# An RWKV-7 scan on one Trainium2 core: two products per step come in the layout of their reader, and the key-side tiles are prepared two steps ahead

## The reference, cut to what matters

```python
def step(S, inp):                       # per head: S is 64 x 64, 16 heads
    r_t, w_t, k_t, v_t, a_t, b_t = inp
    Sa = jnp.einsum('bhvk,bhk->bhv', S, a_t)
    S = S * w_t[:, :, None, :] + Sa[..., None] * b_t[:, :, None, :] + v_t[..., None] * k_t[:, :, None, :]
    y = jnp.einsum('bhvk,bhk->bhv', S, r_t)
    return S, y
_, y = lax.scan(step, S0, (r, w, k, v, a, b))     # 512 tokens
```

## Time and profile before

| | us |
|---|---|
| median of three runs | 1649.29 |
| lowest, highest | 1644.95, 1649.41 |
| the profiled execution's own time | 1648.81 |
| its span in the profile | 1647.0 |
| PE busy (matmuls) | 1545.6, 94% |
| DVE, ACT, POOL busy | 749.6, 586.9, 592.1 |

### The profile page before, as it was taken

How to read it: one execution, slowest core, us unless ns; L and a number is a source line. 1 busy time by engine, 2 the same in 40 slices (tenths; PEclk the granted TensorE clock), 3 DMA queues, 4 the chain that set the end, 5 groups by cost and what they waited for, 6 DMA issues and landing times. The chain is left out here.

```text
span 1647.0 us, 24124 instructions
## 1 busy us (share of the span) xinstructions
PE 1545.6 (94%) x9325; PEld 1205.8 (73%) x9325; DVE 749.6 (46%) x1213; ACT 586.9 (36%) x919; POOL 592.1 (36%) x309
## 2 busy tenths in 40 slices
PE   4699999999899999999999799979999999999998
PEld 3465777777378788888887578745587888888876
DVE  3874969754455320033125773557544310232143
ACT  4655432433333221122234332448442221222242
POOL 4233331110224444434443334244134444344442
PEclk8899999999899999999999999989999999999999
DMA  4121210002212323233323232220022233322331
GB/s 136 51 77 54 92 34 1 3 4 93 79 50 79 102 97 109 92 99 102 103 85 102 78 115 91 77 77 1 1 77 88 91 104 113 102 83 96 102 102 51
DMA packets 123473, 127.33 MB, mean 77 GB/s; under 512 B 8316, under 2 KB 120060, under 8 KB 123384
## 3 DMA queue, kind: packets, MB, share of 16 engines
q1 hardware_dynamic: 122720, 124.90, 23.2%
q0 software_dynamic: 288, 0.59, 0.2%
q10 hardware_dynamic: 376, 0.61, 0.1%
HBM read 123.96 MB, written 2.12 MB: 77 GB/s over the span
## 5 line engine op out<-in xcount | busy, mean ns | idle before, releaser
L439 POOL TENSOR_TENSOR wlo<-wraw,whi 128x1024 fp32r<-128x1024 f32 x108 | 260.6, 2413 | 832.3 <-ACT whi L1223 791.5
L530 PE MATMUL pb<-xh,whi 128*128 128x512 f32 x1184 | 475.7, 402 | 27.9 <-DVE xl L1721 16.3
L531 PE MATMUL pb<-xl,whi 128*128 128x512 f32 x1184 | 464.6, 392 | 0.0
L532 PE MATMUL pb<-xh,wlo 128*128 128x512 f32 x1184 | 464.3, 392 | 0.0
L530 PEld LDWEIGHTS pb<-xh,whi 128*128 128x128 f32 x1184 | 224.2, 189 | 103.4 <-issue 42.3
L1223 ACT ACTIVATE whi<-wraw 128x2048 fp32r<-128x2048 f32 (+1 forms) x111 | 209.2, 1885 | 228.8 <-PE pb L532 223.0
L442 POOL TENSOR_TENSOR wlo<-wraw,whi 128x1024 fp32r<-128x1024 f32 x111 | 274.3, 2471 | 21.1 <-ACT whi L1223 21.1
L531 PEld LDWEIGHTS pb<-xl,whi 128*128 128x128 f32 x1184 | 224.6, 190 | 47.7 <-issue 3.4
L532 PEld LDWEIGHTS pb<-xh,wlo 128*128 128x128 f32 x1184 | 224.4, 189 | 47.8
L530 PE MATMUL pb<-hid_h,whi 128*128 128x512 f32 x512 | 199.3, 389 | 0.0
L531 PE MATMUL pb<-hid_l,whi 128*128 128x512 f32 x512 | 199.2, 389 | 0.0
(11 more groups left out here) (264 smaller groups left out, 1764.5 us busy)
## 6 DMA issues: line engine op xcount, KB each, us to landing
wraw<-in_mlp_w_dram SPq DMA_DIRECT2D x128, 512.0 KB, 4.3
wraw<-in_rwkv_w_rkvo_dram SPq DMA_DIRECT2D x32, 512.0 KB, 4.2
wraw<-in_ple_w_gate_dram SPq DMA_DIRECT2D x16, 512.0 KB, 4.3
xtok<-in_x_dram SPq DMA_DIRECT2D x8, 512.0 KB, 6.6
wraw<-in_w_k_shared_dram SPq DMA_DIRECT2D x8, 512.0 KB, 4.0
wraw<-in_w_v_shared_dram SPq DMA_DIRECT2D x8, 512.0 KB, 4.5
wraw<-in_diff_w_q_dram SPq DMA_DIRECT2D x8, 512.0 KB, 4.0
wraw<-in_diff_w_o_dram SPq DMA_DIRECT2D x8, 512.0 KB, 4.3
```

The source lines that it names most:

```text
L439: pool.tensor_tensor(wlo[:, par, front], wraw[:, par, front], whi[:, par, front].bitcast(F32), ALU.subtract)
L530: mm(o, wh, ah, start=first, stop=False)
L531: mm(o, wh, al, start=False, stop=False)
L532: return mm(o, wl, ah, start=False, stop=last)
```

## The change

What it does:

- Z is computed in the layout in which `solve` reads it, and the state increment in the layout of the state: the operands that are loaded as weights and those that stream change places. `z_taken`, `z_turn`, `h_taken`, `h_turn` and ACT's `decayed` are gone. Because Z, H and Y now differ in which operand is the weights, the product of 192 columns is three of 64 (`value_z`, `value_h`, `value_y`), and `state_in` and `answer` are two of 64 each (`state_z`, `state_y`; `answer_y`, `answer_h`).
- The new state is made by two dependent DVE instructions of 128 columns, increment plus old state and then the decay. In steps 0 and 8 it is one.
- `k_score`, `kv_turn` and their readers work two steps ahead; in the order on PE they alternate with the chain's products.
- `corner` and the value products of the next step alternate two by two.
- In the first half ACT takes the results of `lower_times` and `corner` instead of DVE; `LATE` is spread over fewer steps, so the second inverse ends in step 6 instead of step 7.
- ACT's last `take_u` stands ahead of `high(N_G2, 0)`, and PE's last answer behind the scan's loop. The loads on SP and their conditions stay as they are.

The core of the diff (helpers, semaphore names and the older functions' removed lines are left out):

```diff
+            def value_z(x, k, i):
+
+                if i == 0:
+                    pe.wait_ge(s.kv_ev, k + 1)
+                    pe.wait_ge(s.ll_ev, k + 1)
+                    if k:
+                        pe.wait_ge(s.u_ev[x], k)
+                kv = sets[k % 2][0]
+                for h in range(2):
+                    u, r = 2 * x + i, SWAP[h]
+                    ins = mm(z_part(x, i, ROWS[h]), kv[r, u, 0:CH], kv[r, u, W3:W3 + CH], start=i == 0, stop=False,
+                             skip_group_check=True)
+                if i:
+                    ins.then_inc(s.vz[x], 1)
...
+            def value_y(x, k, i):
+
+                if i == 0 and k:
                     pe.wait_ge(s.y_ev[x], k)
                 kv = sets[k % 2][0]
-                for i in range(2):
+                for h in range(2):
+                    u, r = 2 * x + i, SWAP[h]
+                    ins = mm(y_part(x, i, ROWS[h]), kv[r, u, W3:W3 + CH], kv[r, u, 2 * CH:W3], start=i == 0, stop=False,
+                             skip_group_check=True)
+                if i and k % HALF == HALF - 1:
+                    ins.then_inc(s.vb[x], 1)
...
+            def value_h(x, k, i):
+
+                if k % HALF < HALF - 1:
+                    kv = sets[k % 2][0]
                     for h in range(2):
                         u, r = 2 * x + i, SWAP[h]
-                        if k % HALF < HALF - 1:
-                            ins = mm(zy(x, i, ROWS[h]), kv[r, u, W3:W3 + CH], kv[r, u, 0:W3], start=i == 0, stop=False, skip_group_check=True)
+                        ins = mm(h_part(x, i, ROWS[h]), kv[r, u, CH:2 * CH], kv[r, u, W3:W3 + CH], start=False, stop=False,
+                                 skip_group_check=True)
+                    if i:
+                        ins.then_inc(s.vb[x], 1)
...
+                            pe.wait_ge(s.h_ev[x], later_states(k - 1))
+                    t = units_of(k)[1]
                     for h in range(2):
                         r = ROWS[h]
-                        ins = mm(pb[CB[x]][r, i * CH:(i + 1) * CH], Zt[x][r, i, :], unit(h), start=True, stop=True)
+                        ins = mm(z_part(x, i, r), St[r, LW, pair_of(x, i, k), t], Hs[x][r, k % 2, i, :],
...
+                        mm(y_part(x, i, r), Hs[x][r, k % 2, i, :], St[r, R_, pair_of(x, i, k), t],
+                           start=False, stop=False, skip_group_check=True)
...
+                    ins = mm(u_part(x, i, r), sets[k % 2][1][r, 2 * x + i, :], Zs[x][r, i, :], start=True, stop=True)
+                if i:
+                    ins.then_inc(s.u_mm[x], 1)
...
+                    ins = mm(y_part(x, i, r), Us[x][r, i, :], NL[k // HALF][r, n, CH:P], start=False, stop=True, skip_group_check=True)
...
+                        ins = mm(h_part(x, i, r), NL[k // HALF][r, n, 0:CH], Us[x][r, i, :], start=False, stop=True,
+                                 skip_group_check=True)
...
+            for k in range(NQ):
+                inner, ahead = k + 1 < NQ, k + 2 < NQ
+                state_z(0, k, 0)
+                state_z(0, k, 1)
+                if ahead:
+                    k_score(k + 2, 0)
+                for i in range(2):
+                    if k:
+                        answer_y(1, k - 1, i)
+                    if ahead and i:
+                        k_score(k + 2, 1)
+                for i in range(2):
+                    if k:
+                        answer_h(1, k - 1, i)
+                    if ahead and i:
+                        k_score(k + 2, 2)
+                state_y(0, k, 0)
+                state_y(0, k, 1)
+                if ahead:
+                    k_score(k + 2, 3)
+                value_z(1, k, 0)
+                solve(0, k, 0)
+                value_z(1, k, 1)
+                solve(0, k, 1)
+                for u in range(QUAD):
+                    if inner:
+                        lower_times(k + 1, u)
+                    if ahead and u % 2:
+                        kv_turn(k + 2, u // 2)
+                state_z(1, k, 0)
+                state_z(1, k, 1)
+                if ahead:
+                    kv_turn(k + 2, 2)
+                answer_y(0, k, 0)
+                answer_y(0, k, 1)
+                if ahead:
+                    kv_turn(k + 2, 3)
+                answer_h(0, k, 0)
+                value_y(1, k, 0)
+                answer_h(0, k, 1)
+                value_h(1, k, 0)
+                if inner:
+                    b_turn(k + 1, 0)
+                value_y(1, k, 1)
+                value_h(1, k, 1)
+                if inner:
+                    b_turn(k + 1, 2)
+                    value_z(0, k + 1, 0)
+                    value_z(0, k + 1, 1)
+                solve(1, k, 0)
+                solve(1, k, 1)
+                state_y(1, k, 0)
+                state_y(1, k, 1)
+                if inner:
+                    corner(k + 1, 0)
+                    value_y(0, k + 1, 0)
+                    corner(k + 1, 1)
+                    value_h(0, k + 1, 0)
+                    corner(k + 1, 2)
+                    value_y(0, k + 1, 1)
+                    corner(k + 1, 3)
+                    value_h(0, k + 1, 1)
...
+            pe.wait_ge(s.kv_ev, NQ)
+            spin(F1, 384)
+            spin(F1, 384)
+            answer_y(1, NQ - 1, 0)
+            answer_y(1, NQ - 1, 1)
...
             kv_taken(0)
+            kv_taken(1)
+            lower_taken(0)
+            corner_taken(0)
             b_taken(0)
-            for k in range(NQ + 1):
-                if k:
-                    take_u(1, k - 1)
-                if k < NQ:
-                    decayed(0, k)
-                    take_z(0, k)
+            for k in range(NQ):
+                take_z(0, k)
+                take_u(0, k)
                 if k:
                     take_y(1, k - 1)
-                if k < NQ:
-                    take_u(0, k)
-                kv_taken(k + 1)
-                if k < NQ:
-                    decayed(1, k)
+                lower_taken(k + 1)
+                take_z(1, k)
                 b_taken(k + 1)
-                if k < NQ:
-                    take_z(1, k)
-                    take_y(0, k)
+                take_u(1, k)
+                take_y(0, k)
+                kv_taken(k + 2)
+                corner_taken(k + 1)
                 if k == NQ - 1:
                     for x in range(2):
                         act.wait_ge(s.y_mm[x], NQ - 1)
                     high(N_G2, 0)
+            take_y(1, NQ - 1)
...
-            LATE = ((1, 2, 3), (4, 5)) + tuple((j,) for j in range(6, 27)) + ((27, 28), (29, 30))
+            LATE = ((1, 2, 3, 4), (5, 6), (7, 8)) + tuple((j,) for j in range(9, 23)) + ((23, 24), (25, 26), (27, 28, 29, 30))
...
+            def state(x, k):
 
                 if k % HALF == HALF - 1:
                     return
                 dve.wait_ge(s.y_mm[x], k + 1)
...
+                c = pair_of(x, 0, k) * 8 + k % HALF
+                g = gC[:, c:c + 9:8, None].to_broadcast([P, 2, CH])
+                increment = pb[HY[x]][:, 0:2 * P].rearrange("p (i t) -> p i t", t=P)[:, :, 0:CH]
+                new = Hs[x][:, (k + 1) % 2, :, :]
+                if k % HALF == 0:
+                    tt(new, increment, g, ALU.mult).then_inc(s.grown[x], 1)
+                else:
+                    tt(Hg[x][:, :, :], increment, Hs[x][:, k % 2, :, :], ALU.add).then_inc(s.grown[x], 1)
+                    dve.wait_ge(s.grown[x], states(k))
+                    tt(new, Hg[x][:, :, :], g, ALU.mult).then_inc(s.h_ev[x], 1)
...
             block_pieces(1, 0)
-            lower_taken(0)
+            local_scores(1)
             block_pieces(1, 1)
-            corner_taken(0)
             block_pieces(1, 2)
-            for k in range(NQ + 1):
-                if k < NQ:
-                    z_taken(0, k)
-                    if k == 0:
-                        block_pieces(1, 3)
-                    else:
-                        inverse_late(4 * k - 2)
-                if k:
-                    h_taken(1, k - 1)
-                local_scores(k + 1)
-                if k == 0:
-                    inverse_set(1)
-                else:
-                    inverse_late(4 * k - 1)
-                lower_taken(k + 1)
+            for k in range(NQ):
                 if k:
                     state(1, k - 1)
-                if k < NQ:
-                    inverse_late(4 * k)
-                    z_taken(1, k)
-                    inverse_late(4 * k + 1)
-                    h_taken(0, k)
-                    corner_taken(k + 1)
-                    state(0, k)
+                    inverse_late(4 * k - 4)
+                    inverse_late(4 * k - 3)
+                else:
+                    block_pieces(1, 3)
+                lower_taken(k + 1)
+                state(0, k)
+                if k:
+                    inverse_late(4 * k - 2)
+                else:
+                    inverse_set(1)
+                local_scores(k + 2)
+                if k:
```

(2 more changed lines are left out.)

334 lines of the change are left out of this document (134 added, 200 removed).

## The result

| | us |
|---|---|
| before, median of 20 runs (lowest, highest) | 1649.49 (1644.95, 1651.5) |
| changed, median of 20 runs (lowest, highest) | 1636.55 (1632.04, 1660.09) |
| ratio, 95% interval | 0.9923 [0.9912, 0.9933] |
| profiled execution before, changed | 1648.81, 1637.92 |
| its span before, changed | 1647.0, 1636.1 |

The change is faster by 12.9 us between the medians, where I had forecast 27. The time lies in the range, but near its upper end. The highest of the changed kernel's times, like two more of its 20 (1657.41 and 1658.75), belongs to an execution at a lower mean clock, 0.955 to 0.957 against 0.973 to 0.980, and the ratio is taken without these three.

A forecast was written before the change was run, and what follows sets the result against it. PE's own list was taken as the bound in the second half. Start 292 + 13 x 6.0 + 2.5 + 3.6 + 0.2 = 376.3 against 400.93 gains 24.6; with 1.9 at the end, 26.5 off 1648.81: 1622 us, range 1609 to 1637.

The forecast's parts named there:

- The step, 6.0 us: Scan: PE's list, summed over four sections, takes 6.0 us a step, against 7.19 and 7.76 before.
- 2.5 for DVE: First half of the scan: the second inverse on DVE adds 2.5 us in steps 1, 5 and 6.
- the four sections: PE's step: up to `solve(0)` 1.25, `lower_times` and `kv_turn` 1.08, `state_z(1)` to `state_y(1)` 1.64, `corner` with values 2.03 us.
- The pieces: Scan, `corner`: a piece of two products costs 0.25 us, 0.11 plus 0.14 for the change of row count.
- The rival of dear small pieces (0.36): `corner`: a small piece costs as much as a large one, 0.36 us; 10 us over 13 steps, 1632; chance 0.13.
- the drain in full: PE's row-count changes: each piece 0.07 us longer, 6 us in all, 1628; chance within the dear-pieces rival's.
- The products' order: PE in the scan: products on and off the diagonal overlap; rival of starts only in list order: 13 us, 1635, chance 0.05.
- DVE holds the first half: Rival, first half of the scan: steps 1 to 6 stay at 7.8 us, 1631; chance 0.12.
- The clock: PE's clock would be at 1.00 from step 2 to the end.
- The rival that makes the kernel slower: PE's clock falls to 0.50 and stays low, a step some 5.5 us longer; 1666 if the second half ran so; chance 0.05.
- The start: Start of the scan: the first `state_z` at 292 us, bounds 290 and 295.5.
- Loads and end: Behind the scan: weights split 13.5 us after the first load, first group-norm product about 0.4 after the split's end, 1.9 us gained.

The follow-up runs named there:

- e1: Changed kernel with the four pieces of `corner` in one block and the four value pieces behind it: 1631.81 us, ratio 0.9893.
- e5: e1 with `kv_turn` taking k alone, one product of 128 columns for two of 64, 416 instructions a step: 1627.7 us, ratio 0.9875.
- e4: Changed kernel with each `k_score` product of 128 columns written as two of 64, 480 instructions a step: 1640.6 us, ratio 0.9952.
- e12: Kernel before with each `k_score` product of 128 columns as two of 64, 416 instructions a step for 384: 1649.79 us, ratio 1.0006.
- e6: e1 with `k_score` at 64 columns instead of 128, the same instruction count: 1633.03 us, ratio 0.9903.
- e11: e9 with 44 of DVE's 60 instructions of the second inverse left out: 1629.72 us, ratio 0.9873.
- e2: Changed kernel with the next step's `value_z(0)` put between the two `solve(1)` instead of ahead of them: 1635.58 us, ratio 0.9915.
- e9: Changed kernel with `corner` in one block and ACT's last `take_y` ahead of `high(N_G2, 0)`: 1629.28 us, ratio 0.9872.
- e15: e9 with `high(N_G2, 0)` behind ACT's `centred(2)` and `high(N_WO, 1)` behind `centred(4)`: 1622.61 us, ratio 0.984.
- e7: e1 with the reordering of e2 and with ACT's `b_taken` behind `take_y(0)`: 1633.4 us, ratio 0.9904.
- e13: e9 with one `kv_turn` product for both heads of a pair, four ACT copies of 64 partitions, 416 instructions a step: 1630.97 us, ratio 0.9887.
- e14: e13 with `b_turn` also made for two heads at once, 400 instructions a step: 1639.37 us, ratio 0.9939.
- e16: e13 with ACT's `take_y` ahead of the copies, copies moved into the next step, and e15's end: 1629.76 us, ratio 0.988.
- e17: e16 with `b_turn` for two heads at once as well, 400 instructions a step: 1640.38 us, ratio 0.9948.
- e18: e16 with each `k_score` product as two of 64 columns, 448 instructions a step: 1632.68 us, ratio 0.9905.

## Why the prediction was half right

**The step, 6.0 us: wrong.** This is the term that failed. It was a sum over the array, and the trace of before could carry it, since there the array's own list was the bound: PE at 39.66 of 40 us. Two things stood against it. They overlap, so their shares can't be added.

- *The rate of instructions.* I counted products by their columns and never by their number. 448 instructions in 6.0 us are 75 a us, against 50 in the old scan, a demand 50% above anything the scan had shown. The ceiling is 66, so the mean step can't go under 6.8 (448 / 66), and even a list that fits the array in 6.0 would have lost 0.8 a step. Against the 80.5 us that I had put down for 13 steps (78, and 2.5 for DVE) the measured 13 x 7.13 = 92.7 are 12.2 too many, which is the whole of the missing 12.0. 13 x 6.8 = 88.4 account for 7.9 of them. The waits of e1, its 250 instructions between two of them, e5, and e4 with its control e12 show the ceiling; e6 and e11 agree with it. The Trainium skill (Runtime: NRT & Kernel Launch, Terms and the note on TENSOR_LOAD) says that an engine's instructions lie in a memory of its own that is refilled in blocks of 16 KiB, by a fetch that runs by itself; the trace agrees on the block, 0.41 MB in 25 packets. How fast the blocks come is told by the runs here alone.
- *The array's own time* is 6.47 us in the undisturbed step, not 6.0; by itself it would have cost 13 x 0.47 = 6.1 us. It lies under the floor of 6.8, but not by much, which fits the mere 3.9 us of waits for issue in the changed kernel. By the four sections: start 1.36 for 1.25 (365.93 to 367.29), `lower_times` 1.08 for 1.08, third 2.12 for 1.64 (368.37 to 370.49), `corner` 1.91 for 2.03. In the third, `solve(1)` and `state_y(1)` start only when the `value_z` ahead of them in the list are nearly through: I had let products of the two kinds run past each other without limit. The rows show the overlap, but not over so many products. e2, which shortens just this queue, gained nothing measurable; the rate above it is a reason, but no run shows that it is the only one.

**The pieces: right.** 0.25 us, as the line through the larger pieces said. The rival of dear small pieces (0.36) is refuted, and so is the drain in full. But the alternation wasn't free: 1 us of array time a step, of which the supply let e1 win back a quarter.

**The products' order: right.** `state_z` starts at 368.39, 0.02 us after the `kv_turn` ahead of it at 368.37; starts strictly by the list were no bound here either.

**DVE: right in its ops.** The transposes began at 333.0 and 335.0 us (forecast: done near 330). A state instruction takes 0.292 us (0.33 forecast). Steps k = 1 to 7 take 7.44 us on the mean, those from 9 to 14 6.90. The rival "DVE holds the first half" (7.8) is nearer to the first number than the forecast is, and without e11 I should have believed it.

**The clock: right in the second half only.** It was lower in 292 to 298 (0.72) and 338 to 342 us (0.57), and again at 400 to 410 (0.50), and came back each time; I had it at 1.00 from step 2 on. From 342 us to the end of the scan it was. The rival that makes the kernel slower didn't occur, and that owes something to luck: in e4 and e9 the clock stood at 0.66 for 10 us of the scan.

**The start: right.** First `state_z` at 294.0 against 292, and these 2 us lie ahead of the scan.

**Loads and end: 1.9 forecast, 2.2 measured.** The split comes 13.1 us after the first load (13.5 forecast), the first group-norm product 15.50 after it, 17.68 before: 2.2 us. About 1.1 of it is given back, as the group norm starts at the low clock: its second `centred` stands 3.55 us behind the first, before 2.41. PE is idle for 7.9 us ahead of it, where it was for 5.66 in the kernel before, and I priced only the gain. I had also ended the term at the split: e15 shows that 9.2 us more lay in ACT's list behind it (2.5 with e9, not clear of noise by itself, and 6.7 with e15).

**Together.** 24.6 forecast to the first load and 12.6 measured, the difference all in the step; 1.9 forecast behind it and 2.2 - 1.1 measured. The profiled execution ends 10.9 us earlier: 12.6, less the 2 us ahead of the scan, plus 1.1, is 11.7, and the last 0.8 I haven't traced. That the time still lies in the range is no merit of the sum: no rival in it was about the number of instructions, and its bounds came from other dangers, which didn't occur.

**Open.** What limits the fetch of instructions to 25 blocks in 100 us no run here tells. That the packets are PE's blocks is inferred from the count, some 250 instructions to each, and from their beat. What the changed kernel would take with a faster supply and nothing else different isn't measured either; its issue waits sum up to 3.9 us. Nor was a kernel found with the whole computation that both stays under the rate and keeps ACT off the path, so what the array alone would need isn't measured.

## What to carry to other kernels

Count an engine's instructions per step beside its array time, before and after a change, and take the number per us as a resource of its own: a product cut in three has the same columns on the array and three times the instructions. "issue" waits that wander over the lines, at the beat of the instruction queue's packets, are its sign. Once the rate is used up, further orders (e7 over e1), fewer columns (e6) or freeing another engine (e11) gained nothing here; fewer instructions shortened the step (e5), as long as their price on another engine is small, which it wasn't in e13, e14, e16 and e17. And where a list holds a wait for a load, move everything whose inputs are there ahead of it: that was worth 9.2 us here, against 4.7 for the best order in the scan (e1).

## What the hardware showed that I had not expected

- In the scan PE was given at most 25 blocks of 16 KB in 100 us, some 66 instructions a us on the mean, though it took 74 to 83 a us between two waits (e1): enough for products of 128 columns, too little for a list of 64-column ones.
- The same 32 instructions a step cost 4 us where the rate was used up (e4) and nothing where it wasn't (e12).
- ACT copies 64 partitions x 256 elements in 0.38 us, and 128 x 256 (`b_taken`) in 0.38 as well: to work on half the partitions saved no time there. Four such copies take the place of one of 128 x 512, 0.61 us, in e13, e14 and e16 to e18. PE's waits for ACT sum up to 7.3 us in e14 and 8.7 in e17, over 295 to 375 us.
